# First projection's products of seven y tiles placed inside the last steps of the attention, with buffers shared by the two phases

## The reference

```python
for layer in range(DEPTH):                       # DEPTH = 2
    hnorm = rms_norm(x, mixer_norm[layer])
    if layer % 2 == 0:
        x = x + attention_mixer(hnorm, ...)      # ends with  y @ w_out
    else:
        x = x + mlstm_mixer(hnorm, ...)
    x = x + sq_relu_mlp(rms_norm(x, mlp_norm[layer]), mlp_w_in[layer], mlp_w_out[layer])
# in attention_mixer: 16 heads of 64, groups (window, dilation) = (128,1), (512,4), (2048,16)
y = einsum('gbsh,gbshe->bshe', softmax_over_groups(lses), outs)
return y.reshape(b, s, 1024) @ w_out             # the "first projection"
```

## Time and profile before

| what | value |
| --- | --- |
| median of 3 runs | 3260.49 us (3259.43 to 3260.71) |
| the profiled execution's own time | 3261.04 us |
| its span, first to last instruction | 3259.3 us |
| PE busy in the span | 3109.3 us (95%) |
| mean granted TensorE clock | 0.978 |
| DVE, ACT, POOL busy | 1297.3, 1104.6, 927.6 us |
| DMA over the span | 201.85 MB, mean 62 GB/s |

### The profile page before, as it was taken

How to read it: one execution, slowest core, us unless ns; L and a number is a source line. 1 busy time by engine, 2 the same in 40 slices (tenths; PEclk the granted TensorE clock), 3 DMA queues, 4 the chain that set the end, 5 groups by cost and what they waited for, 6 DMA issues and landing times. The chain is left out here.

```text
span 3259.3 us, 44365 instructions
## 1 busy us (share of the span) xinstructions
PE 3109.3 (95%) x16134; PEld 2689.9 (83%) x16134; DVE 1297.3 (40%) x3508; ACT 1104.6 (34%) x3122; POOL 927.6 (28%) x787
## 2 busy tenths in 40 slices
PE   6999999999999958999999999999788999999999
PEld 5999999999999946788888887778566788888887
DVE  5556556565555643422223133520263422213131
ACT  3565656565555533211111123111263211111110
POOL 5444444444444312222222222122202222222221
PEclk9999999999999968999999999999898999999999
DMA  3222222222222214111111111111111111111112
GB/s 123 60 66 81 76 77 77 72 85 66 82 78 75 60 38 168 46 46 52 46 51 47 50 48 46 39 46 56 60 40 52 46 52 46 52 46 52 46 52 78
DMA packets 143125, 201.85 MB, mean 62 GB/s; under 512 B 29611, under 2 KB 109118, under 8 KB 142910
## 3 DMA queue, kind: packets, MB, share of 16 engines
q1 hardware_dynamic: 140606, 194.81, 19.0%
q10 hardware_dynamic: 2304, 4.20, 0.3%
HBM read 173.25 MB, written 25.70 MB: 61 GB/s over the span
## 5 line engine op out<-in xcount | busy, mean ns | idle before, releaser
L69 PE MATMUL ps_qk<-w_hi,attn_hT_hi 128*128 128x384 f32 x1536 | 536.5, 349 | 25.5 <-POOL w_lo L851 13.5
L71 PE MATMUL ps_qk<-w_hi,attn_hT_lo 128*128 128x384 f32 x1536 | 517.2, 337 | 0.0
L70 PE MATMUL ps_qk<-w_lo,attn_hT_hi 128*128 128x384 f32 x1536 | 516.5, 336 | 0.0
L928 POOL TENSOR_TENSOR first_w_lo<-first_raw,first_w_hi 128x1024 fp32r<-128x1024 f32 x96 | 231.3, 2409 | 855.3 <-ACT first_w_hi L924 855.3
L928 POOL TENSOR_TENSOR second_w_lo<-second_raw,second_w_hi 128x1024 fp32r<-128x1024 f32 x72 | 172.1, 2391 | 620.1 <-ACT second_w_hi L924 620.1
L69 PEld LDWEIGHTS ps_qk<-w_hi,attn_hT_hi 128*128 128x128 f32 x1536 | 290.1, 189 | 31.2 <-DVE attn_hT_lo L662 26.0
L70 PEld LDWEIGHTS ps_qk<-w_lo,attn_hT_hi 128*128 128x128 f32 x1536 | 291.0, 189 | 0.0
L71 PEld LDWEIGHTS ps_qk<-w_hi,attn_hT_lo 128*128 128x128 f32 x1536 | 290.0, 189 | 0.0
L69 PE MATMUL first_ps<-first_hid_hi,first_w_hi 128*128 128x512 f32 x640 | 250.7, 392 | 32.7 <-DVE first_hid_lo L1254 32.6
L892 POOL TENSOR_TENSOR rs<-var,minus_half 128x4 f32<-128x4 f32 x192 | 193.3, 1007 | 271.9 <-DVE var L740 271.8
L69 PE MATMUL first_ps<-first_hT_hi,first_w_hi 128*128 128x512 f32 x640 | 252.8, 395 | 14.2 <-POOL first_w_lo L928 14.2
(11 more groups left out here) (258 smaller groups left out, 6134.2 us busy)
## 6 DMA issues: line engine op xcount, KB each, us to landing
raw<-in_wqkv SPq DMA_DIRECT2D x192, 192.0 KB, 2.4
first_raw<-in_w SPq DMA_DIRECT2D x64, 512.0 KB, 3.2
second_raw<-in_w SPq DMA_DIRECT2D x64, 512.0 KB, 3.2
v_dram<-v_out SPq DMA_DIRECT2D x192, 64.0 KB, 1.5
w_bc<-share_dram SPq DMA_DIRECT2D x48, 256.0 KB, 4.3
v_raw<-v_dram SPq DMA_DIRECT2D x32, 256.0 KB, 3.0
first_raw<-in_vo_pieces SPq DMA_DIRECT2D x16, 512.0 KB, 3.2
bias<-bias_dram SPq DMA_DIRECT2D x16, 256.0 KB, 3.3
```

The costliest lines, as they stand in the source:

```text
L69: pe.matmul(out, a_hi, b_hi, start=first, stop=False)
L70: pe.matmul(out, a_hi, b_lo, start=False, stop=False)
L71: return pe.matmul(out, a_lo, b_hi, start=False, stop=last)
L928: pool.tensor_tensor(self.lo[:, n % 2, :], self.raw[:, n % self.RAW, :], self.hi[:, n % 2, :].bitcast(F32), ALU.subtract).then_inc(self.lo ...
```

## The change

Attention and first dense phase now share buffers and PSUM banks, so that the first projection can begin while the attention is ending. The attention's own input (`attn_hT_hi`, `attn_hT_lo` before) now lies in the dense phase's `hid_hi` and `hid_lo`; `FirstProjection` owns the weight stream, which lies over the weights of the even sections. Once the last q, k, v product is made, those places are free.

1. The weights. SP loads pieces 0 and 1 of the projection in step 186, 2 and 3 in step 193, 4 and 5 in step 209. ACT and POOL split pieces 0 and 1 in steps 188 and 190, piece 2 in step 203, piece 3 in step 208 (`first.high`, `first.low`). Since the last y tile comes late, the 128 columns of pieces 0 to 3 that meet it are kept apart (`w7_hi`, `w7_lo`).
2. The y tiles. SP loads tiles 0 to 6 from DRAM in step 192, ACT makes their high parts in steps 193 to 199, DVE the low parts in steps 194 to 200. Tile 7 is no longer stored: ACT and DVE split it straight from SBUF in step 213.
3. The products. PE makes k tiles 0 to 6 of outputs 0, 1, 2 (9 products per step) in steps 195 to 201, and in step 202 those of output 3, of 4 and 5, and of 6 and 7 (105 products). Eight banks hold the open sums across the barrier.
4. x and the gains are loaded by SP in step 193.
5. The dense phase starts with the 3 products of k tile 7 for outputs 0 to 3, and takes the others in the order 8, 4, 9, 5, 10, 6, 11, 7, 12, 13, 14, 15. Its ACT list begins with pieces 4 and 5. The last y store and the eight y loads after the barrier are gone.

```diff
+    def low(self, pool, n):
+        raw = self.stream.raw[:, n % 2, (KT - 1) * P:KT * P]
+        pool.wait_ge(self.w7_hi_done, n + 1)
+        pool.tensor_tensor(self.w7_lo[:, n, :], raw, self.w7_hi[:, n, :].bitcast(F32), ALU.subtract).then_inc(self.w7_lo_done, 1)
+        self.stream.low(pool, n)
...
@@ attention, SP
+                if st == SECTIONS - 1 and j == 2:
+                    sp.wait_ge(qk_mm, TT * (SECTIONS - 1))
+                    first.load(sp, 0)
+                    first.load(sp, 1)
+                if st == SECTIONS and j == 0:
+                    sp.wait_ge(qk_mm, TT * SECTIONS)
+                    sp.wait_ge(y_out, 16 * (PAIRS - 1))
+                    for k in range(KT - 1):
+                        sp.dma_start(y_lo[:, k, :].bitcast(F32), yT_dram[k]).then_inc(y_in[k], 16)
...
@@ attention, PE
+                def project(outputs, ks):
+                    for k in ks:
+                        pe.wait_ge(y_lo_done, k + 1)
+                        for i in outputs:
...
+                            c0 = (i % 2) * HALF
+                            wk_hi, wk_lo = first.stream.block(i // 2, k)
+                            mm = split_matmul(pe, banks[i][:], wk_hi, wk_lo, y_hi[:, k, c0:c0 + HALF], y_lo[:, k, c0:c0 + HALF],
+                                              k == 0, False)
+                            if k == KT - 2 and i % 2 == 1:
+                                mm.then_inc(piece_used, 1)
...
+                if TT * SECTIONS + 3 <= T < TT * SECTIONS + 3 + KT - 1:
+                    project((0, 1, 2), [T - TT * SECTIONS - 3])
+                if st == SECTIONS + 1 and j == 2:
+                    project((3,), range(KT - 1))
+                    project((4, 5), range(KT - 1))
+                    project((6, 7), range(KT - 1))
...
@@ attention, ACT
+                if st == SECTIONS - 1 and j in (4, 6):
+                    first.high(act, j // 2 - 2)
+                if st == SECTIONS and 1 <= j:
+                    act.wait_ge(y_in[j - 1], 16)
+                    act.copy(y_hi[:, j - 1, :], y_lo[:, j - 1, :].bitcast(F32)).then_inc(y_hi_done, 1)
+                if st == SECTIONS + 1 and j == 3:
+                    act.wait_ge(piece_used, 1)
+                    first.high(act, 2)
+                if st == LAST_SUPER and j == 0:
+                    act.wait_ge(piece_used, 2)
+                    first.high(act, 3)
+                if st == LAST_SUPER and j == 5:
+                    act.wait_ge(y_step, 5 * PAIRS)
+                    act.copy(y_hi[:, KT - 1, :], o_raw[0][:, (PAIRS - 1) % 2, :]).then_inc(y_hi_done, 1)
...
@@ dense_block
+        outs = (0, 1, 2, 3, 8, 4, 9, 5, 10, 6, 11, 7, 12, 13, 14, 15) if begun else tuple(range(2 * KT))
...
+                if begun and i < PROJECTED:
+                    mm = split_matmul(pe, bank(key)[:], first.w7_hi[:, n, :], first.w7_lo[:, n, :],
+                                      hid_hi[:, KT - 1, cols], hid_lo[:, KT - 1, cols], False, True)
```

More of the change, by code:

```diff
@@ L114, in phase_semaphores @@
 @contextmanager
-def phase_semaphores(nc, prefix):
-    made = []
+def phase_semaphores(nc, prefix, earlier=()):
+    made = list(earlier)
     def sem(name):
@@ L892, in step @@
                     pool.tensor_tensor(rs[:], var[:], minus_half[:, 0:4], ALU.pow).then_inc(rs_done, 1)
+                if st == SECTIONS - 1 and j in (4, 6):
+                    first.low(pool, j // 2 - 2)
+                if st == SECTIONS + 1 and j == 3:
+                    first.low(pool, 2)
+                if st == LAST_SUPER and j == 0:
+                    first.low(pool, 3)
             run_supersteps(step)
@@ L1119, in _ @@
         def _(pool):
-            for n in range(MIX0):
+            for n in range(EARLY if begun else 0, MIX0):
                 stream.low(pool, n)
@@ L1169, in _ @@
                     n = MLP0 + 2 * KT * c + q
-                    stream.high(act, n + 1)
+                    if not begun or n > MLP0:
+                        stream.high(act, n + 1)
                     if c == 0 and q == 0:
@@ L1234, in sum_tile @@
             def sum_tile(stage, m):
-                d, half = divmod(m, 2)
+                d, half = final_output(stage, m)
                 cols = half_cols(half)
                 count = 2 * KT * stage + m
+                again = m >= 1 and final_output(stage, m - 1)[1] == half
                 dve.wait_ge(h_hi_done, count + 1)
@@ L1428, in _ @@
                             if c == 0:
-                                user = max(i for i in range(len(order)) if i % 8 == t)
-                                pe.wait_ge(freed, read(order[user]))
+                                pe.wait_ge(freed, read(users[t]))
                             elif c <= VO_CHUNKS // 2:
@@ L1844, in trunk @@
         total = ctx.enter_context(nc.sbuf_tensor("total", [P, SEQ], F32, side="right"))
-        with ExitStack() as first:
-            buffers = AttentionBuffers(nc, first)
-            hT_hi, hT_lo = first.enter_context(split_hidden(nc, "attn"))
-            attention_phase(nc, ones, ident, buffers, total, mixer_gain[0], hT_hi, hT_lo, xT_in, rel_bias, onehot, wqkv, q_gain, k_gain,
-                            bias_dram, yT_dram)
+        buffers = AttentionBuffers()
+        with ExitStack() as below:
+            buffers.below_x(nc, below)
         xT = ctx.enter_context(nc.sbuf_tensor("xT", [P, KT, SEQ], F32, side="right"))
@@ L1852, in trunk @@
             gates = cell.enter_context(nc.sbuf_tensor("mlstm_gates", [P, TT, 2 * MH], F32))
-            with ExitStack() as dense:
+            with ExitStack() as early:
+                hid = hidden_buffers(nc, early, "first")
+            with ExitStack() as below:
+                buffers.below_first(nc, below)
+            qk = cell.enter_context(nc.sbuf_tensor("mlstm_qk", [P, QK_PIECES, SEQ], F32))
+            v1 = cell.enter_context(nc.sbuf_tensor("mlstm_v1", [P, TT, MH, VW], F32))
+            with ExitStack() as dense:
+                mix = Mixer(nc, dense, qk, v1, gates, og_dram, gate_w, conv_w, conv_b)
+                with ExitStack() as below:
+                    buffers.below_stream(nc, below)
+                first = FirstProjection(nc, dense, xT_in, xT, attn_wo, mlp_gain[0], mixer_gain[1])
+                banks = [dense.enter_context(nc.psum_tensor(f"first_ps{i}", [P, HALF], F32)) for i in range(8)]
+                attention_phase(nc, ones, ident, buffers, first, banks, total, mixer_gain[0], hid[0], hid[1], xT_in, rel_bias, onehot,
+                                wqkv, q_gain, k_gain, bias_dram, yT_dram)
                 rstd = dense.enter_context(nc.sbuf_tensor("first_rstd", [P, SEQ], F32, side="right"))
```

304 lines of the change are left out of this document (181 added, 123 removed).

## The result

| | before | changed |
| --- | --- | --- |
| median of 4 runs | 3260.60 us (3259.43 to 3261.26) | 3213.13 us (3211.84 to 3214.18) |
| the profiled execution's own time, and its span | 3261.04, 3259.3 us | 3214.14, 3212.4 us |
| mean granted clock | 0.978 | 0.986 |

The ratio is 0.9854, with a 95% interval of 0.9842 to 0.9866: 47.5 us less, where 46 were forecast (3214.5 us, range 3211 to 3220).

A forecast was written before the change was run, and what follows sets the result against it. PE idling at the attention's end and before the barrier was taken as the bound. Projection end moves from 1327.1 to 1280.8, 46.3 us off 3261.04, giving 3214.7, or 3214.2 from the median; stated 3214.5, range 3211 to 3220.

The forecast's parts named there:

- the likeliest case: Whole kernel: the forecast itself, 3214.5 us, own range 3212 to 3217.5, chance 0.78.
- saving from W to A: From step 191's first weighing to the last output added to x: 46.3 us less, the projection ending at 1280.8.
- The steps: Steps 195 to 201: nine products at low clock 3.9 us, then full-clock steps of 3.55, the last two 3.0 and 2.7.
- The casts of pieces 0 and 1: Steps 188 and 190: weight casts on ACT and POOL fit into gaps while PE is full, costing nothing.
- The barrier: Between step 202's products and the dense phase: costs 1.0 us, upper bound 4.3 us.
- The wait for piece 4: Ahead of output 8, behind the barrier: PE waits 1.0 us for the cast and low part.
- The price put on a fall: Behind the barrier, as upper bound: 8 products of 0.43 instead of 0.23 us, 1.7 us.
- The cover: Ahead of the barrier: y tile 7 ready at 1224.8, five microseconds before PE is done.
- The merge as the barrier's setter: Rival at y tile 7: chain over 5.0 us late decides the barrier; 8 us late gives 3219.2; chance 0.11.
- The steps did not stay at the low clock: Denies a rival for steps 195 to 201: low clock, 6.35 us per step, 15 us late, 3229.5; chance 0.05.
- The placement: Rival: new SBUF placement lengthens each of 192 attention steps; at 0.35 us per step 3282; chance 0.03.
- The filling: Steps 195 to 201: products fill them; rival, inputs too late, all 168 behind step 201, 3227.9, chance 0.03.

The follow-up runs named there:

- e1_behind: Changed kernel with the 63 products of outputs 0 to 2 moved from steps 195 to 201 to the head of step 202; 3228.44 us.
- e2_late84: Changed kernel with the 84 products of outputs 4 to 7 made behind the barrier instead of in step 202; 3230.86 us.
- e6_tile7_dram: Changed kernel with y tile 7 stored to DRAM and loaded back instead of split from SBUF; 3218.19 us.
- e3_merge_2: Changed kernel with two idle DVE additions of 1.25 us each inside the last merge; 3212.63 us.
- e4_merge_8: Changed kernel with eight idle DVE additions of 1.25 us each inside the last merge; 3219.27 us.
- e7_piece4: Changed kernel with weight piece 4 cast ahead of the barrier, in step 213, instead of behind it; 3214.40 us.
- e12_again: The same kernel as e10_both, run once more; 3211.59 us.
- e9_warm2: Changed kernel with useless PE products ahead of two pauses in step 192 and at the end of steps 193 and 194; 3214.39 us.
- e10_both: Changed kernel with the edits of e9_warm2 and e7_piece4 together; 3211.16 us.

## Why the prediction was right

The forecast was 3214.5 us, the median is 3213.13, inside the likeliest case's own range. The cause is the one forecast: the products lie where PE idled, and PE instead of the merge reaches the barrier last. That the saving from W to A agrees to the tenth is luck: terms that are off by 0.3 to 1.1 us cancel. To compare by its steps, 1.14 us has to be added to the times of the changed trace, since its W lies that much earlier than in the trace on which the sum was made:

| step | predicted | measured + 1.14 |
| --- | --- | --- |
| projection products of step 195 start | 1182.1 | 1182.75 |
| full clock from | 1186.0 | 1186.6 |
| step 202 begins | 1206 | 1205.49 |
| y tile 7 ready | 1224.8 | 1225.45 |
| step 202's products done (0.2267 us behind the last one's start) | 1229.8 | 1229.29 |
| PE resumes | 1230.8 | 1230.77 |
| output 8 begins | 1234.5 | 1234.33 |
| projection ends (PE) | 1280.8 | 1280.8 |
| saving from W to A | 46.3 | 46.3 |

**What bounds it.** Right: e1_behind brings the old steps of 4.01 us, with their pauses, back. Beside e1_behind (15.0 us) and e2_late84 (16.4), what the start at the full clock and the store and loads that are gone give is not held apart by a run, except for the store and load of tile 7 (e6_tile7_dram, 2.6).

**The steps.** Right in kind, with two errors that cancelled. The nine products of step 195 took 3.85 us at the low clock, 3.9 predicted, and the clock rose where predicted. A full step took 3.42 us, not 3.55: PE's own work in it is 3.42 - 2.04 = 1.38 us, for which 1.5 was estimated, and the last two took 2.93 and 2.41 us instead of 3.0 and 2.7. From the rise on that is 18.9 us where 20.0 were put: 1.1 too much. Also, PE issues the first projection product 0.34 us before the turned probabilities are done.

**The casts of pieces 0 and 1, "nothing".** This was wrong by 1.0 us, the other error: it is why step 195 starts later than predicted. Step 192's weighing comes 4.05 us behind W, and 3.08 before (1166.37 - 1163.29). Timelines of POOL, DVE, ACT and PE in the changed kernel:

```profile
1159.84 2.40 POOL L1059 TENSOR_TENSOR first_w_lo<-first_raw,first_w_hi 128x1024 fp32r<-128x1024 f32 x1 [0.49 <-ACT first_w_hi L192]
```

```profile
1160.11 2.14 DVE L820 TENSOR_SCALAR neg_max<-stat 128x2 f32<-128x2 f32 x1
```

```profile
1162.29 0.37 ACT L653 ACTIVATE prob<-first_ps,neg_max 128x128 f32<-128x128 f32 x1 [2.53 <-DVE neg_max L820]
```

```profile
1165.91 0.41 PE L489 MATMUL first_ps<-ident,qkn 128*128 128x128 f32 x2 [1.76 <-DVE qkn L874]
```

This DVE instruction, of two elements per partition, has a median of 0.17 us over the 192 of them; this one took 2.14 us and ended at 1162.25, with POOL's low part of piece 1 (1162.24). It is so in all thirteen traces with this cast, and no `neg_max` of the kernel before took over 0.5 us. The exponential and all behind it moved, and PE waited 1.76 us where it had waited 0.90 before. Piece 0, in step 188, does the same to its `neg_max` (1148.11, 2.14 us), but there PE has q, k and v products to make and nothing is lost: the cover that was named in the prediction is gone exactly where piece 1 needs it. The prediction looked for this contention only at instructions with two SBUF inputs, and `neg_max` has one. The Trainium skill, SBUF — State Buffer, section SBUF: two separate sides, calls the shared ports an exclusive lock: whichever of the DVE instruction (in a 2-port mode, or with two SBUF inputs) and the GpSimd one starts first has them for its whole length, and the other blocks. The trace agrees in the times, 2.14 us for 0.17 and both ends together; whether `neg_max` ran in such a mode the profile does not show. Casting piece 1 elsewhere was not tried, so the 1.0 us are read from the traces and not from a run.

**The barrier.** 1.0 us was taken, from the barrier behind the mLSTM cell. It is 1.33 us of idle time, and 1.32 to 1.33 us from the end of the last work in each of e2_late84, e3_merge_2, e4_merge_8 and e6_tile7_dram, whichever engine came last: mis-sized by 0.3 us, or by 0.5 where, as in the table, the last product is counted with 0.2267 us; under the 4.3 us bound.

**Behind it.** The wait for piece 4 is 0.57 us idle and was priced at 1.0; the longer barrier does not shorten it, since both start there. The two pauses cost no clock, as predicted. The price put on a fall, 1.7 us, is borne out: e4_merge_8 loses 1.2 from R to A although the pause ahead of output 8 is gone, 1.8 with it put back.

**The cover** was given as 5.0 us and is 4.0, by the changed trace and by what e2_late84, e4_merge_8 and e6_tile7_dram used up. One merge, L951, took 2.46 us beside POOL's 2.40, 1.2 more than in the earlier trace rows; two such delays had been priced at 3.6 in all. In e7_piece4 tile 7's low part took 2.58 us instead of 1.22. The cover held both.

**The rivals.** The merge as the barrier's setter would have needed 4.0 us more. Its price holds roughly: for a tile 10.5 us late the prediction's rule (less 5.0 of cover, plus 1.7 for the clock) gives 7.2 us, and e4_merge_8 lost 7.7 from W to A. The steps did not stay at the low clock. The placement did not lengthen the attention (1000 of 1000 us busy, 6657 products in the window against 6650). The filling did happen; e1_behind, which has all 168 products behind step 201, is the case that the prediction put at 3227.9, and took 3228.44.

**The last step, from A to the end,** was taken as unchanged. It is 1932.6 against 1932.1 us here, and anything from 1929.7 to 1933.9 in the others, so the 1.4 us between forecast and median say nothing of the changed part.

## What to carry to other kernels

Where two phases meet, work of the second that needs only finished inputs can fill the first's drain; its worth is the products that move, and it stops where another chain, here the merge with 4.0 us to spare, reaches the barrier first. So find the slack of that chain before moving more, and measure it by padding (two additions free, eight at 7.7 us). A transfer or cast that is moved into gaps must be laid against the smallest instructions of the other engine, not only the large ones. Fillers that were to keep the clock gained nothing behind the first pauses and 3.4 us ahead of them, and even there not in every execution. Gains under 2 us are read as distances between two fixed instructions, since the start alone moves by 3 us from one execution to the next.

## What the runs showed of the hardware

- The clock falls or does not fall at the same pause of the same PE work. The 3.14 us pause in the MLP, released by POOL, was followed by a product of 0.50 us and no low clock in the changed kernel, by one of 0.80 us before, and in e12_again by 14 at the low clock, the first of them 0.79 us; the first additions to x behind it came 71.1, 72.6 and 73.9 us after this product. The same two pauses of 0.75 and 0.57 us led to a fall in e9_warm2 and to none in e10_both and e12_again.

```profile
1306.39 0.50 PE L69 MATMUL first_ps<-first_hT_hi,first_w_hi 128*128 128x512 f32 x1 [3.14 <-POOL first_w_lo L1059]
```

- A fall can come after PE has resumed: in e6_tile7_dram five products ran at the full clock behind a pause of 3.29 us, then about eight at the low one. The 1.33 us of the barrier, where PE came last to it, brought no fall in any of ten traces.
- DVE beside POOL does not slow down in proportion to its size: 0.17 us of work took 2.14 and 1.23 us took 2.46. L951 starts at 1211.66, POOL's instruction ends at 1213.04, and L951 ends at 1214.12, 1.1 us behind that: nearly as if it had begun only then. In e7_piece4 tile 7's low part starts at 1225.35, POOL's cast ends at 1226.84, and the low part ends at 1227.93, again 1.1 us behind.
- A store queued behind large loads waits for them. In the changed kernel SP issued the small store of the last maxima (16 KB) at 1180.54, behind 8.9 MB, and the loads that wait for it could issue at 1192.58; it landed 12.0 us after its issue. DVE used the maxima only from 1200.9 on, so nothing was lost; on a shorter last stretch it would be the next bound. Timeline of SP:

```profile
1172.30 6.00 SPq L440 DMA_DIRECT2D xT<-in_xT_in  x8
...
1180.54 1.08 SPq L392 DMA_DIRECT2D stat_dram<-stat_rows  x1
1192.58 2.61 SPq L401 DMA_DIRECT2D compact<-stat_dram  x4
```
